# Cache moves issued by ScalarE during the projection instead of by SyncE during prompt attention

## The chip, the cores and the metric

The kernel runs on one core of a Trainium2 chip. The metric is the device time of one execution in microseconds. The core has five engines that run their own instruction streams and meet only through semaphores: TensorE (PE; its weight loads are shown apart, as PEld), VectorE (DVE), ScalarE (ACT), GpSimd (POOL) and SyncE (SP, used only to issue DMAs). 16 DMA engines move the data; each issuing engine has a queue of its own for them (q1 is SyncE's, q10 ScalarE's, q0 GpSimd's).

## The reference

One decoder layer is run for a prompt of 512 tokens and for 8 samples of 4 new tokens each that share the weights. All tokens are normed and multiplied by one wide matrix, `w_in`; its columns are the queries, keys and values of a sparse attention (NSA) and of three dilated attention groups, and the merge gates. Attention over the prompt, attention of the samples over their caches, an output projection and a mixture of experts follow.

What matters here is the last thing that the layer returns: every sample's window caches, shifted by the four new tokens (of the dilated groups; the NSA window is treated alike):

```python
buf = jnp.concatenate([dil_caches[g][l], jnp.stack([k, v], axis=2)], axis=1)
...
dil_s[g].append(buf[:, -n_buf:])
```

Rows 4 to w of each cache go unchanged to rows 0 to w-4 of the output. This copy depends on nothing that the layer computes. It is 46.9 MB in all: for one sample 4088 KB (2048 window), 1016 KB (512), 248 KB (128) and 508 KB (NSA window).

## The kernel before

The kernel is written engine by engine: within a stage, a `Block`, each engine has its own list of instructions, and every order between engines is a semaphore written out by hand. The engines meet at the end of a block. The stages that matter, in order of time:

- **Norm and transpose** (0 to 30 us). Beside it SyncE loads x, the first two chunks of `w_in` and tables; ScalarE loads a gain and the identity matrix (L598, L599).
- **Projection**, `project` (30 to 243 us). The columns of `w_in` up to the merge gates are cut into 11 chunks of 328 columns. Chunks come in pairs: `u` is 0 or 1, `k` counts the turns; a loop of 5 turns does both, and one chunk follows it. For each chunk SyncE loads 1312 KB in rows of 1312 bytes (L299, `load`), into one of two buffers `w[:, u]`; it waits until the chunk before in the same `u` is multiplied. VectorE splits the chunk into an upper part and a rest (L112 and L116, called by `split`). TensorE multiplies five token tiles (four of 128 tokens, one of 32) with three products each (L122 to L124), into eight PSUM banks used round and round. ScalarE and VectorE copy the banks into `rows` in turns (`copies`, L346; ScalarE the even ones: three copies in a chunk of `u` 0, two in one of `u` 1).
- **Merge gates and rotation**, `finish_rows` (243 to 370 us): the last 2048 columns in 16 loads of 512 KB, with the rows' rotation beside them.
- **Prompt attention**, `prompt_nsa` (370 to 552 us) and `prompt_dilated` (552 to 663 us).
- **Sample attention**, the mixing and the experts, whose weights are the largest traffic of the kernel.

The order inside VectorE's loop in `project` matters for the steps below:

```python
with dve.Fori(0, TURNS) as i:
    split(1, i)
    copies(dve, 1, dve.tensor_copy, s_dve, 0, i)
    split(0, i + 1)
    copies(dve, 1, dve.tensor_copy, s_dve, 1, i)
```

Before a chunk with `u` 0, TensorE waits for all copies of the turn before on both engines (`s_act` and `s_dve` at 5k).

The cache moves are DMAs from DRAM to DRAM, made by `move_cache` (L567 to L576; its DMA stands as L574 in the profile). It lays one sample's window out as (pieces, y) with y of at most 1024 elements. SyncE issues them: in `prompt_nsa` two samples' 2048 window in each of four turns of its loop, in `prompt_dilated` the other three windows of four samples in each of two turns. Nothing waits for them but the end of the kernel (`s_moved`, L2706).

Of the kernel before, what the change touches and what calls it, by code (L numbers as in the profile page):

```python
# [12 lines left out]
TP, BS, SS = 512, 8, 4  # L13
# [4 lines left out]
HD, NH, KVH, REP = 64, 8, 2, 4  # L18
# [64 lines left out]
CREDIT = 1  # L83
# [27 lines left out]
def upper_part(dve, out, src):  # L111
    return dve.tensor_copy(out, src)  # L112


def rest_part(dve, out, whole, upper):
    return dve.tensor_tensor(out, whole, upper, ALU.subtract)  # L116


def product_of_parts(pe, out, lhsT, rhs, first, last):

    a, b = lhsT, rhs
    pe.matmul(out, a[0], b[0], start=first, stop=False)  # L122
    pe.matmul(out, a[0], b[1], start=False, stop=False)  # L123
    return pe.matmul(out, a[1], b[0], start=False, stop=last)  # L124
# [6 lines left out]
class Program:  # L131
# [144 lines left out]
    def project(self, hT, hT_rest, w, wu, wr, s_w, rows, src, tables_loaded):  # L276

        nc = self.nc  # L280
        w_in = self.i["w_in"][0]
        TURNS = C_MRG // WCH // 2
        KV_TURNS = -(-(C_KC + 4 * HD) // (2 * WCH))
        with ExitStack() as s:
            acc = self.ps(s, "proj_acc", [P, 8, 512])
            s_up = self.lsem("w_in_upper_ready")
            s_sp = self.lsem("w_in_split")
            s_mm = [self.lsem(f"proj_accumulated{u}") for u in range(2)]
            s_act = self.lsem("proj_copied_by_act")
            s_dve = self.lsem("proj_copied_by_dve")  # L290
            s_src = self.lsem("compressor_source_copied")
            self.s_mw = [self.sem(f"merge_w_loaded{j}") for j in range(MERGE_RING)]
            self.credit()
            with nc.Block() as block:
                @block.sync
                def _(sp):
                    def load(u, k):
                        sp.wait_ge(s_mm[u], (NT + 1) * k + CREDIT)
                        sp.dma_start(w[:, u, :, :], w_in[:, bass.ds((2 * k + u) * WCH, WCH)]  # L299
                                     .rearrange("(k p) c -> p k c", p=P)).then_inc(s_w[u], 16)  # L300

                    with sp.Fori(0, TURNS - 1) as i:
                        load(0, i + 1)
                        load(1, i + 1)
                    load(0, TURNS)
                    for m in range(MERGE_RING):
                        self.load_merge_w(sp, m)
                    sp.wait_ge(s_act, 5 * KV_TURNS + CREDIT)
                    sp.wait_ge(s_dve, 5 * KV_TURNS + CREDIT)
                    for t in range(NT):  # L310
                        for kg in range(4):
                            c = C_KC + kg * HD
                            sp.dma_start(src[8 * t:8 * t + 8, kg], rows[:, t, c:c + HD]).then_inc(s_src, 16)
                    sp.wait_ge(s_src, 16 * 4 * NT + CREDIT)
                    tables_loaded(sp)

                @block.tensor
                def _(pe):
                    def chunk(u, k):
                        pe.wait_ge(s_sp, 2 * k + u + 1 + CREDIT)  # L320
                        if u == 0:
                            pe.wait_ge(s_act, 5 * k + CREDIT)
                            pe.wait_ge(s_dve, 5 * k + CREDIT)
                        for t in range(NT + 1):
                            n = 5 * u + t
                            if n >= 8:
                                pe.wait_ge((s_act, s_dve)[(n - 8) % 2], 5 * k + (n - 8) // 2 + 1 + CREDIT)
                            tok = slice(t * P, t * P + ROWS[t])
                            for c in range(KD):
                                ins = product_of_parts(pe, acc[:ROWS[t], n % 8, 0:WCH],  # L330
                                                       (hT[:, c, tok], hT_rest[:, c, tok]),
                                                       (wu[:, u, c, :], wr[:, u, c, :]), c == 0, c == KD - 1)
                            ins.then_inc(s_mm[u], 1)

                    with pe.Fori(0, TURNS) as i:
                        chunk(0, i)
                        chunk(1, i)
                    chunk(0, TURNS)

                def copies(eng, which, copy, done, u, k):  # L340

                    for t in range(NT + 1):
                        n = 5 * u + t
                        if n % 2 == which:
                            eng.wait_ge(s_mm[u], (NT + 1) * k + t + 1 + CREDIT)
                            copy(rows[:ROWS[t], t, bass.ds((2 * k + u) * WCH, WCH)],  # L346
                                 acc[:ROWS[t], n % 8, 0:WCH]).then_inc(done, 1)

                @block.scalar
                def _(act):  # L350
                    with act.Fori(0, TURNS) as i:
                        for u in range(2):
                            copies(act, 0, act.copy, s_act, u, i)
                    copies(act, 0, act.copy, s_act, 0, TURNS)

                @block.gpsimd
                def _(pool):
                    self.bias_steps[0](pool)

                @block.vector  # L360
                def _(dve):
                    def split(u, k):

                        dve.wait_ge(s_w[u], 16 * k + 16 + CREDIT)
                        upper_part(dve, wu[:, u], w[:, u]).then_inc(s_up, 1)
                        dve.wait_ge(s_up, 2 * k + u + 1 + CREDIT)
                        rest_part(dve, wr[:, u], w[:, u], wu[:, u]).then_inc(s_sp, 1)

                    split(0, 0)
# [5 lines that stand above are left out]
                    copies(dve, 1, dve.tensor_copy, s_dve, 0, TURNS)  # L375
# [409 lines left out]
    def prompt_nsa(self, rows, qrot, kcT, vc, o_tok):  # L785
# [9 lines left out]
        with ExitStack() as s:  # L795
# [22 lines left out]
            s_qt = self.lsem("pn_q_transposed")  # L818
# [19 lines left out]
            with nc.Block() as block:  # L838
# [80 lines left out]
                @block.sync  # L919
                def _(sp):  # L920
                    sp.dma_start(self.ks[:, :], self.c["sample"]).then_inc(s_ks, 16)
                    sp.wait_ge(s_z, 1 + CREDIT)
                    for i in range(NT):
                        sp.dma_start(vcz[32 * i:32 * i + NC, i, :], vc[:, :]).then_inc(s_vz, 16)
                    with sp.Fori(0, REP) as r:
                        sp.wait_ge(s_qt, 2 * r + 2 + CREDIT)
                        for j in range(BS // REP):
                            self.move_cache(sp, "cache_dil_w2048", "dil2048_sample", BS // REP * r + j)
                    sp.wait_ge(s_ks, 16 + CREDIT)

                @block.gpsimd
# [116 lines left out]
    def prompt_dilated(self, rows, o_tok):  # L1048
# [6 lines left out]
        with ExitStack() as s:  # L1055
# [13 lines left out]
            s_qt = self.lsem("pd_qk_transposed")  # L1069
# [16 lines left out]
            with nc.Block() as block:  # L1086
                @block.sync
                def _(sp):
                    with sp.Fori(0, 2) as jp:
                        sp.wait_ge(s_qt, 6 * jp + 6 + CREDIT)  # L1090
                        for j in range(BS // 2):
                            for src, dst in (("cache_dil_w512", "dil512_sample"), ("cache_dil_w128", "dil128_sample"),
                                             ("cache_nsa_win", "nsa_win_sample")):
                                self.move_cache(sp, src, dst, BS // 2 * jp + j)
                    sp.wait_ge(self.s_rows_out, 16 * self.n_rows_out)

                @block.gpsimd
# [1855 lines left out]
```

## Time and profile before

| | us |
|---|---|
| median of 3 runs | 1530.58 |
| lowest and highest run | 1524.55, 1533.27 |
| the profiled execution | 1536.05 |
| its span, first to last instruction | 1534.2 |
| TensorE busy in the span | 1211.8 (79%) |
| VectorE, ScalarE, GpSimd busy | 519.4, 296.9, 112.5 |
| data moved by DMA | 280.05 MB |

How to read it: "busy" is the time in which an engine has an instruction under way; the DMA share is the mean busy share of the 16 DMA engines; the granted clock of TensorE is given as a share of full speed, 1.00 for 2.4 GHz and 0.50 for 1.2 GHz. A packet is what the trace records as one piece of a transfer on one DMA engine; the completion of a DMA adds one small packet for each engine. A DMA's "landing" is counted from its issue to the semaphore that says that all of it has arrived. An idle engine costs nothing unless something on the path waits for it.

### The profile page before, as it was taken

What the parts mean: (1) busy time and instruction counts of PE and PEld (TensorE: products, weight loads), DVE (VectorE), ACT (ScalarE), POOL (GpSimd) and SP (SyncE); (2) the same over time, 40 slices, a digit from 0 to 9 for tenths busy, and PEclk for the clock granted to TensorE, in tenths of its full rate; (3) what the DMA queues carried; (4) which work ended last, traced back from release to release, by engine and by line L of the source; (5) the groups of instructions that cost most, each with busy time, mean ns of one, the idle gap of its engine ahead of it and who ended that gap; (6) DMA issues with size and microseconds to landing.
All of it is one profiled execution on the core that took longest, in us unless ns stands there. A gap on an engine that the chain in (4) does not pass through costs nothing. (4 is left out here: it accounts for less than half of the span.)

```text
span 1534.2 us, 21060 instructions
## 1 busy us (share of the span) xinstructions
PE 1211.8 (79%) x7946; PEld 913.0 (60%) x7946; DVE 519.4 (34%) x1053; ACT 296.9 (19%) x652; POOL 112.5 (7%) x173
## 2 busy tenths in 40 slices
PE   3999998996887777887649966995799749988760
PEld 2999998996666656646528754865575423333320
DVE  6222323141555545543413243234231341101105
ACT  3000002311333322312203222232001101101102
POOL 1400005000000020000000000000000001111100
PEclk9999999898799989967769987997799859999985
DMA  7122242263666632525652222220572369999955
GB/s 223 48 84 80 70 91 67 88 189 107 220 218 218 218 122 69 189 110 220 274 219 111 111 96 126 111 110 0 219 254 125 140 254 419 423 424 423 425 222 188
DMA packets 74629, 280.05 MB, mean 183 GB/s; under 512 B 16772, under 2 KB 45216, under 8 KB 61728
## 3 DMA queue, kind: packets, MB, share of 16 engines
q1 hardware_dynamic: 66144, 231.55, 41.3%
q0 software_dynamic: 5824, 42.48, 6.9%
q10 hardware_dynamic: 2592, 5.05, 0.9%
q8 instruction: 49, 0.80, 0.2%
q14 instruction: 20, 0.16, 0.0%
HBM read 264.80 MB, written 69.53 MB: 218 GB/s over the span
## 5 line engine op out<-in xcount | busy, mean ns | idle before, releaser
L122 PE MATMUL proj_acc<-w_in_upper,hT_upper 128*128 128x328 f32 (+1 forms) x440 | 139.2, 316 | 10.9 <-DVE w_in_rest L116 7.1
L2519 PE MATMUL ex_up_ps<-ex_w_up,ex_hT 128*64 128x512 f32 x512 | 125.2, 645 | 28.1 <-DMA ex_w_up<-in_expert_w_up 27.1
L123 PE MATMUL proj_acc<-w_in_rest,hT_upper 128*128 128x328 f32 (+1 forms) x440 | 139.1, 316 | 0.0
L124 PE MATMUL proj_acc<-w_in_upper,hT_rest 128*128 128x328 f32 (+1 forms) x440 | 138.1, 314 | 0.0
L722 PE MATMUL sn_hp<-sn_xT,cmp_w 128*128 128x127 f32 x1024 | 118.2, 275 | 0.0
L722 PEld LDWEIGHTS sn_hp<-sn_xT,cmp_w 128*128 128x128 f32 x1024 | 116.2, 192 | 0.0
L2519 PEld LDWEIGHTS ex_up_ps<-ex_w_up,ex_hT 128*64 128x64 f32 x512 | 41.5, 148 | 100.6 <-issue 90.1
L122 PEld LDWEIGHTS proj_acc<-w_in_upper,hT_upper 128*128 128x128 f32 (+1 forms) x440 | 76.7, 174 | 16.0 <-issue 12.6
L122 PE MATMUL merge_ps<-hT_upper,merge_w_upper 128*128 128x272 f32 x256 | 77.7, 303 | 4.1 <-DVE merge_w_rest L116 4.1
L123 PEld LDWEIGHTS proj_acc<-w_in_rest,hT_upper 128*128 128x128 f32 (+1 forms) x440 | 76.8, 175 | 3.6
L124 PEld LDWEIGHTS proj_acc<-w_in_upper,hT_rest 128*128 128x128 f32 (+1 forms) x440 | 76.7, 174 | 3.7
L123 PE MATMUL merge_ps<-hT_rest,merge_w_upper 128*128 128x272 f32 x256 | 77.0, 301 | 0.0
L124 PE MATMUL merge_ps<-hT_upper,merge_w_rest 128*128 128x272 f32 x256 | 76.8, 300 | 0.0
L2540 PE MATMUL ex_down_ps<-ex_w_down,ex_actT 128*64 128x512 f32 x256 | 58.4, 597 | 2.0 <-DMA ex_w_down<-in_expert_w_down 1.4
L2614 DVE TENSOR_TENSOR ex_act<-ex_silu,ex_up_ps 128x256 f32<-128x256 f32 x16 | 6.7, 421 | 155.2 <-ACT ex_silu L2570 155.2
L2051 PE MATMUL mx_ps<-mx_w_out,mx_mixT 128*128 128x512 f32 x128 | 56.2, 594 | 1.0 <-DVE mx_products L2142 1.0
L895 PE MATMUL pn_O<-rows,pn_pT 128*128 128x128 f32 x320 | 44.6, 288 | 13.8 <-DVE pn_pT L1003 13.8
L863 PE MATMUL pn_S<-pn_kT,pn_qT 128*128 128x128 f32 (+3 forms) x128 | 51.0, 514 | 5.0 <-ACT pn_qT L951 5.0
L122 PEld LDWEIGHTS merge_ps<-hT_upper,merge_w_upper 128*128 128x128 f32 x256 | 51.5, 201 | 4.6 <-DVE merge_w_rest L116 4.4
L895 PEld LDWEIGHTS pn_O<-rows,pn_pT 128*128 128x128 f32 x320 | 39.5, 197 | 23.4 <-DVE qrot_and_o_tok L1040 18.9
L2039 PE MATMUL mx_ps<-oT,mx_w 128*128 128x272 f32 x192 | 45.9, 403 | 8.2 <-DMA mx_w<-in_w_branch_dil 8.2
L124 PEld LDWEIGHTS merge_ps<-hT_upper,merge_w_rest 128*128 128x128 f32 x256 | 51.6, 201 | 0.0
(429 smaller groups left out, 1945.3 us busy)
## 6 DMA issues: line engine op xcount, KB each, us to landing
ex_w_up<-in_expert_w_up SPq DMA_DIRECT2D x32, 2048.0 KB, 28.0
ex_w_down<-in_expert_w_down SPq DMA_DIRECT2D x32, 1024.0 KB, 35.7
out_dil_sample<-in_cache_dil_w SPq DMA_DIRECT2D x8, 4088.0 KB, 21.4
sd_kv<-in_cache_dil_w SPq DMA_DIRECT2D x16, 1024.0 KB, 11.8
w_in_chunk<-in_w_in SPq DMA_DIRECT2D x11, 1312.0 KB, 5.7
merge_w<-in_w_in SPq DMA_DIRECT2D x16, 512.0 KB, 5.1
out_dil_sample<-in_cache_dil_w SPq DMA_DIRECT2D x8, 1016.0 KB, 10.1
merge_gates_scratch<-qT_dil ACTq DMA_DIRECT2D x16, 272.0 KB, 4.2
```

What stands on the lines that cost most here:

```text
L122: pe.matmul(out, a[0], b[0], start=first, stop=False)
L123: pe.matmul(out, a[0], b[1], start=False, stop=False)
L124: return pe.matmul(out, a[1], b[0], start=False, stop=last)
L722: ins = pe.matmul(b["hp"][kg % 2][:, 0:n - 1], self.w1[:, kg // 2, j, :], b["xT"][:, kg % 2, j % 8, j // 8:j // 8 + n - 1], start=j == 0, ...
L863: pe.matmul(S[bf][:, j, 0:n], qT[:, 1, g, i * P:(i + 1) * P], kT[:, j, 0:n], start=True, stop=False)
L895: pe.matmul(O[u % 2][:, j * P:(j + 1) * P], pT[:, j, kb * P:(kb + 1) * P], rows[:, kb, c:c + KVD], start=kb == 0, stop=kb == i)
L2039: ins = pe.matmul(ps[:, 4 * (m % 2) + 2 * p + half, 0:HT], w[:, c0 + k, m * P:(m + 1) * P], oT[:, c0 + k, half * HT:(half + 1) * HT], star ...
L2051: ins = pe.matmul(ps[:, n % 3, :], mixT[:, k, t * P:(t + 1) * P], wo[:, k, half * 512:(half + 1) * 512], start=k == 0, stop=k == KD - 1)
L2519: ins = pe.matmul(up_ps[r, q, :], hT[:, q, c, r], wu[slot][:, u, c, :], start=c == 0, stop=c == KD - 1)
L2540: ins = pe.matmul(dn_ps[r, half, :], aT[:, q, c, r], wd[slot][:, u, c, half * 512:(half + 1) * 512], start=c == 0, stop=c == 1)
L2614: dve.tensor_tensor(ac[:, q, :], sl[:, q, :], up_ps[:, q, FF:2 * FF], ALU.mult).then_inc(s_ac, 1)
```

## The change

ScalarE issues all 32 moves, on its own queue, in the projection: four DMAs (one sample) ahead of each group of copies, for the first eight chunks. Its loop has four turns instead of five, and the fifth is written out. The two loops of moves on SyncE are gone. `move_cache` is as before and is called with ScalarE in the place of SyncE. The number of moves, the data and the final wait are the same.

```diff
--- before.py
+++ after.py
@@ -348,9 +348,16 @@
 
                 @block.scalar
                 def _(act):
-                    with act.Fori(0, TURNS) as i:
+                    MOVED = (("cache_dil_w2048", "dil2048_sample"), ("cache_dil_w512", "dil512_sample"),
+                             ("cache_dil_w128", "dil128_sample"), ("cache_nsa_win", "nsa_win_sample"))
+                    with act.Fori(0, BS // 2) as i:
                         for u in range(2):
+                            for from_cache, to_cache in MOVED:
+                                self.move_cache(act, from_cache, to_cache, 2 * i + u)
                             copies(act, 0, act.copy, s_act, u, i)
+                    for k in range(BS // 2, TURNS):
+                        for u in range(2):
+                            copies(act, 0, act.copy, s_act, u, k)
                     copies(act, 0, act.copy, s_act, 0, TURNS)
 
                 @block.gpsimd
@@ -922,10 +929,6 @@
                     sp.wait_ge(s_z, 1 + CREDIT)
                     for i in range(NT):
                         sp.dma_start(vcz[32 * i:32 * i + NC, i, :], vc[:, :]).then_inc(s_vz, 16)
-                    with sp.Fori(0, REP) as r:
-                        sp.wait_ge(s_qt, 2 * r + 2 + CREDIT)
-                        for j in range(BS // REP):
-                            self.move_cache(sp, "cache_dil_w2048", "dil2048_sample", BS // REP * r + j)
                     sp.wait_ge(s_ks, 16 + CREDIT)
 
                 @block.gpsimd
@@ -1086,12 +1089,6 @@
             with nc.Block() as block:
                 @block.sync
                 def _(sp):
-                    with sp.Fori(0, 2) as jp:
-                        sp.wait_ge(s_qt, 6 * jp + 6 + CREDIT)
-                        for j in range(BS // 2):
-                            for src, dst in (("cache_dil_w512", "dil512_sample"), ("cache_dil_w128", "dil128_sample"),
-                                             ("cache_nsa_win", "nsa_win_sample")):
-                                self.move_cache(sp, src, dst, BS // 2 * jp + j)
                     sp.wait_ge(self.s_rows_out, 16 * self.n_rows_out)
 
                 @block.gpsimd
```

## Rows read from the trace of the kernel before

**Rows 1.** busy us (share of the span) and instructions by engine, from the page.
```profile
PE 1211.8 (79%) x7946; PEld 913.0 (60%) x7946; DVE 519.4 (34%) x1053; ACT 296.9 (19%) x652; POOL 112.5 (7%) x173
```

**Rows 2.** busy time in stretches: projection, merge gates, prompt attention, experts.
```profile
core 0: us, PE busy (x) PEld busy (x) DVE busy (x) ACT busy (x) POOL busy (x), PEclk, DMA share, GB/s
30.00:243.00 213.00, 202.19 (x1320) 189.67 (x1320) 63.80 (x49) 12.10 (x29) 22.70 (x20) 1.00 0.24 71
243.00:370.00 127.00, 122.71 (x940) 122.03 (x940) 41.18 (x69) 29.84 (x59) 22.71 (x60) 0.93 0.41 123
370.00:552.00 182.00, 135.61 (x856) 107.85 (x856) 93.28 (x301) 61.01 (x181) 8.58 (x12) 0.87 0.58 194
1255.00:1492.00 237.00, 203.74 (x918) 78.30 (x914) 26.92 (x47) 28.71 (x63) 31.74 (x37) 0.94 0.91 380
```

**Rows 3.** waits of TensorE from 370 to 663 us: total us, times, longest.
```profile
PE pn_O L895 <- DVE pn_pT L1003: 13.8, 12, 1.4
PE pn_O L909 <- DVE pn_cmp_exp L1024: 12.8, 4, 3.2
PE pn_PT L854 <- DMA pn_cmp_v_by_tile<-prompt_vc: 8.1, 1, 8.1
```

**Rows 4.** timeline of ScalarE in the projection: start us, us, what [idle before].
```profile
56.02 0.42 ACT L346 COPY rows<-proj_acc 32x328 f32 x1 [6.75 <-PE proj_acc L124]
70.45 0.43 ACT L346 COPY rows<-proj_acc 128x328 f32 x1 [6.75 <-PE proj_acc L124]
78.66 0.43 ACT L346 COPY rows<-proj_acc 128x328 f32 x1 [7.77 <-PE proj_acc L124]
115.69 0.43 ACT L346 COPY rows<-proj_acc 128x328 f32 x1 [7.79 <-PE proj_acc L124]
```

**Rows 5.** timeline of VectorE in the projection, the split of one chunk.
```profile
61.82 1.53 DVE L112 CAST w_in_upper<-w_in_chunk 128x2624 fp32r<-128x2624 f32 x1 [8.85 <-DMA w_in_chunk<-in_w_in]
63.38 2.89 DVE L116 TENSOR_TENSOR w_in_rest<-w_in_chunk,w_in_upper 128x2624 fp32r<-128x2624 f32 x1
```

**Rows 6.** the loads of w_in by line: issue ns, first, last start; landing.
```profile
L299 SPq DMA_DIRECT2D w_in_chunk<-in_w_in x9: 372/373/397, 56.1 to 204.0; - x9
DMA to landing us min/median/max: 5.6/5.7/6.0
```

**Rows 7.** the Exp of prompt attention, 471-497 us, then 497-508 us.
```profile
L959 ACT ACTIVATE pn_exp<-pn_S,pn_stats x13: 358/474/689, 472.7 to 496.9; 128x128 f32<-128x128 f32 x4, 128x256 f32<-128x256 f32 x4, 128x384 f32<-128x384 f32 x3, 128x512 f32<-128x512 f32 x2
...
L959 ACT ACTIVATE pn_exp<-pn_S,pn_stats x4: 572/630/688, 496.9 to 500.9; 128x384 f32<-128x384 f32 x2, 128x512 f32<-128x512 f32 x2
```

**Rows 8.** the moves by line; the first two in the queue's timeline.
```profile
L574 SPq DMA_DIRECT2D out_dil_sample<-in_cache_dil_w x24: 520/521/657, 385.0 to 621.0; - x24
...
384.96 1.52 SPq L574 DMA_DIRECT2D out_dil_sample<-in_cache_dil_w  x2
```

**Rows 9.** SyncE's queue, 384-415 us, 562-588 us; one us after an issue.
```profile
q1 hardware_dynamic: 160, 8.37, 82.5%
...
q1 hardware_dynamic: 384, 7.26, 83.5%
...
384.90:385.90 1.00, 0.00 (x0) 0.00 (x0) 0.37 (x1) 0.99 (x2) 0.98 (x2) 0.50 0.00 0
```

**Rows 10.** SyncE's queue, 57 to 62 us: packets, MB, share of 16 engines.
```profile
q1 hardware_dynamic: 1040, 1.34, 77.2%
```

**Rows 11.** both queues, 6.5 to 7.5 us: packets, MB, share of 16 engines.
```profile
q1 hardware_dynamic: 99, 0.36, 89.5%
q10 hardware_dynamic: 98, 0.05, 16.4%
```

**Rows 12.** busy time and granted clock (after POOL) around a pause of TensorE.
```profile
912.00:925.80 13.80, 0.18 (x1) 0.00 (x0) 11.35 (x13) 2.12 (x2) 0.79 (x1) 0.50 0.96 411
925.80:931.80 6.00, 5.37 (x45) 4.48 (x49) 1.96 (x6) 1.17 (x2) 0.00 (x0) 0.50 0.90 388
931.80:936.00 4.20, 3.71 (x125) 3.04 (x116) 0.35 (x1) 0.00 (x0) 0.00 (x0) 1.00 0.02 4
```

## The prediction

> **What bounds the kernel now.** I read the busy time and the clock by stage first. TensorE is busy over the whole span for 79% [rows 1], but the stage that receives the moves is tighter than that: in the projection (30 to 243 us) it works 202 of 213 us at the full clock, while the DMA engines are used to 24%; in prompt attention (370 to 552 us), from which the moves are taken, it works 136 of 182 us, with the DMA engines at 58%; the experts (1255 to 1492 us) are the only stage that the DMA engines bound, at 91% [rows 2]. So transfers are to go from a stage where an engine has idle time into one where TensorE has almost none. The question is then what each stage waits for.
>
> In prompt attention the waits of TensorE name other engines: 13.8 us for VectorE's probabilities, 12.8 us for the compressed ones. The one DMA wait, 8.1 us, is for a small load that TensorE needs before the loop in which the moves stand [rows 3]. No wait names a cache move.
>
> In the projection one turn of the loop (two chunks of w_in) takes 37.03 us: ScalarE's first copy of a turn stands at 78.66 and again at 115.69 us [rows 4]. A chunk is five token tiles of 3.6 us (two of ScalarE's copies, two tiles apart, are 7.2 us apart). The load of the chunk after next is issued as a chunk ends (56.1 us; the last copy of that chunk starts at 56.02), lands 5.7 us later, and VectorE splits it in 4.4 us (61.82 to about 66.2 us) [rows 4 to 6]. It is needed at 75.0 us (the copy at 78.66 less one tile of 3.6). So a load has 8.8 us of cover at most, and it can take up to about 14.5 us from issue to landing before TensorE notices. That cover is what the change uses.
>
> **Part by part.** *Taken from SyncE.* 8 moves of the 2048 window in prompt attention and 24 smaller ones in the dilated part, with their two waits. SyncE has nothing else to do there, and nothing else is queued behind them (the next load of its queue is issued after the moves have landed). What this gives back: nothing on the path. The Exp of 128x512 takes at most 689 ns with moves under way (471 to 497 us) and 688 ns without (497 to 508 us) [rows 7], so the attention's engines are not slowed by them. Bounds: 0 to 5 us, taken 0; zero is what these rows are nearest to.
>
> *Given to ScalarE, the issuing.* Four DMAs ahead of each of the first eight groups of copies. SyncE needs 0.52 us for one issue, and some 0.25 us of register work lies between two of them (two issues in 1.52 us) [rows 8]: about 3.1 us a group. ScalarE sits idle 6.75 to 7.79 us before every copy [rows 4], so this is hidden: 0. Behind the issues stand the copies that free the PSUM banks; without the cover it would be 8 x 3.1 = 25 us, and that would need the queue to push back. Seven packets a queue and sample, below, speak against it. The peeled turn has the same copies as the looped one: 0.
>
> *The transfers themselves.* This is the term that decides, and it needs the size of packets. Two 2048 moves are 160 packets, 8.37 MB; 32 of the packets are the 16 completions of each, so 128 packets carry 65 KB each, 8 on each of 16 engines. They use the engines for 82.5% of 31 us = 25.6 us, so 3.2 us a packet. Four samples' smaller moves (12 DMAs) are 384 packets, 192 of them data, 3 an engine and sample, and use 83.5% of 26 us = 21.7 us, 5.4 us a sample [rows 9]. One sample is thus 4 + 3 = 7 large packets and 4 x 3.2 + 5.4 = 18.2 us of every DMA engine; eight samples are 146 us. A load of w_in is 1024 data packets of 1312 bytes, 64 an engine, in 77.2% of 5 us = 3.9 us, 0.06 us a packet [rows 10]. Both together, 22.1 us, are already more than a chunk of 18.5 us.
>
> How two queues share an engine is seen at 6.5 to 7.5 us, where ScalarE's queue (512-byte rows of the identity) and SyncE's (4 KB rows of x) are both full: 98 packets of one and 99 of the other in 1 us, 0.05 against 0.36 MB [rows 11]. So they take turns packet by packet, whatever the size. Beside the moves a w_in packet of 0.06 us then waits for a move packet of 3.2 us. A load gets 64 turns only if the moves end before.
>
> **One turn, followed.** Times are those of the turn at 56 us. The load is issued at 56.1 and its first packet runs 1.3 us later (5.7 less 3.9, less 0.5 for the completion), at 57.4. ScalarE ends its last copy at 56.4, issues at about 56.7, and the first move packet runs at 58.0, if it needs the same 1.3 us (no byte moved in the first 0.9 us after such an issue [rows 9]). Ten packets of the load are through by then. The sample's 7 packets last until 58.0 + 18.2 + 0.4 = 76.6 us, and 7 of the load pass with them. But ScalarE issues the next sample after its copy at 70.45 us [rows 4], at about 71.2, and these packets stand ready at 72.5, 4 us before the queue would run dry. So 7 more packets of moves go first, until 95.2 us; the load has had 24. The other 40 take 2.4 us: it lands at 98.1. VectorE splits until 102.5, then makes the three copies that stand behind the split in its order (1.6 us; TensorE waits for them before a new turn), and TensorE starts at 104.1 instead of 75.0 us: **29.1 us** lost. The other chunk's load, queued behind, lands at 102 and is split by 108.5, ahead of 122, so it costs nothing. The third sample is issued only after the delayed chunk, so that the next turn repeats this from its own start. This holds for three turns; in the fourth only one sample (the eighth) stands against the load: the moves end at 76.6 in the same frame, the load, 47 packets short, lands at 79.9, and TensorE starts at 85.9: 10.9 us. Sum 3 x 29.1 + 10.9 = **98 us**.
>
> *The clock.* After 13.8 us in which TensorE did almost nothing the granted clock was 0.50, the 1.2 GHz level, and it stayed there for the first 6.0 us of work before it returned to 2.4 GHz [rows 12]. At half speed that is 3 us for each long stall, 9 us, and I take 2 for the short one: **11 us**.
>
> *The rest.* The first sample is issued at about 30 us, when no load of w_in is on its way; it stretches the compressor's weight loads, for which only GpSimd waits, long before the merge stage needs its product: 0. The last sample is through before the ninth chunk starts, so the merge stage (96% busy [rows 2]) and its loads meet no moves: 0. Later stages are as before.
>
> The sum is +109 us: 1536.05 us for the profiled execution (its span is 1534.2) becomes 1645, and on the median of the runs, 1530.58, **1640 us**.
>
> **Rivals.** (1) The queues take turns, but the load gets through in a few turns. Against it are the 98 and 99 packets of [rows 11]; for it, that this row has packets of at most 4 KB. If it waited for four move packets, it would land at about 58.0 + 12.8 + 3.2 + 0.5 = 74.5 and TensorE start at 80.5, 5.5 us late; four turns, each with something for the second load too, are 15 to 35 us. If it waited for one sample but never for two (were the moves 25% faster, the queue would run dry first), it is 4 x 11 + 8 = 52 us. So 1546 to 1583 us, about 1560 in the middle. The Trainium skill has such a rule: "DMA: Bandwidth & Descriptors", section "Queues, rings and completion order", says that an engine drains a packet of typically 9 to 17 descriptors from one ring before it switches. If each packet of this trace were one of its descriptors, an estimate from that page is four to six turns for a load, the first of these two cases. The trace at 6.5 to 7.5 us shows one for one and does not agree.
>
> (2) The load is hardly delayed: the large packets are cut up and bytes are shared fairly. A load of 3.9 us then takes about 8 and lands within 10 us of its issue, inside the 14.5. Then TensorE sees nothing, and what the moves lag behind (8 x (22.1 - 18.5) = 29 us) is absorbed by the last three chunks. 1531 to 1536, about 1533 us. Against it: nothing in the rows shows a packet interrupted, and the moves' packets keep an engine 3.2 us each, one behind the other.
>
> (3) Faster: the moves do cost something in prompt attention that its waits do not name. The place is the first 26 us of each of its four turns and the 22 us after each issue of the small moves; were the chain 5% slower there, it would be 4 x 1.3 + 2 x 1.1 = 7.4 us, 1523 us, and only if rival 2 held as well. It decides from about 5% on. The two equal Exp durations speak against it [rows 7].
>
> (4) The moves don't run there at all, because ScalarE's queue takes them late: with seven packets an engine and sample there is no reason. It would end as rival 2 and has no chance of its own.
>
> **The numbers.** My forecast 0.65, with 1605 to 1670 of its own (a stall of 25 to 33 us, with and without the clock); rival 1 0.20; rival 2 0.10; rival 3 0.05. The range takes the forecast's upper end and most of rival 1: 1555 to 1670 us. About 0.5%, 7.7 us, is what a measurement of this kernel can tell from no change. Faster by more: 0.04; within: 0.11; slower: 0.85.
>
> **What would show it.** Right: in the projection, TensorE waits of some 29 us, three times, and one of 11, put down to VectorE's copies or split, which wait for the w_in load; landing of every second w_in load at about 42 us instead of 5.7; a granted clock of 0.50 after each stall; packets of 65 KB on ScalarE's queue (q10), 46.9 MB there; ScalarE's issues at 0.5 us each; prompt attention within 2 us of before. Wrong: w_in loads that land in under 14 us (then rival 2), or in about 18 (rival 1); issues on ScalarE of many us each, with its copies late (then the issuing was the term that I set at 0); a shorter prompt attention (rival 3). The sum hangs on the next sample's being issued 4 us before the queue runs dry; a small shift there is worth 18 us a turn.

## The result

| | before | changed |
|---|---|---|
| median of the runs (4 each) | 1529.84 us | 1637.41 us |
| range of the runs | 1524.55 to 1533.27 | 1634.94 to 1638.95 |
| ratio to before, 95% interval | 1 | 1.0683 [1.0657, 1.071] |
| span of the profiled execution | 1534.2 us | 1635.7 us |

The changed kernel is 7% slower: 107.6 us by the medians, 101.5 us by the spans of the two profiled executions (that of before lay some 6 us above its median).

The page of the changed kernel, busy time and queues:

```profile
PE 1212.1 (74%) x7946; PEld 915.2 (56%) x7946; DVE 517.1 (32%) x1053; ACT 296.6 (18%) x652; POOL 111.3 (7%) x173
...
q1 hardware_dynamic: 64736, 183.54, 30.1%
q10 hardware_dynamic: 4000, 53.05, 9.3%
```

TensorE is busy for as long as before [rows 1]; only its share has fallen. The moves now stand on q10, which carried 5.05 MB before; the 48.0 MB between are the 46,880 KB of 1024 bytes that the text ahead of the prediction calls 46.9 MB. By stretches (projection, merge gates, the two parts of prompt attention):

```profile
core 0: us, PE busy (x) PEld busy (x) DVE busy (x) ACT busy (x) POOL busy (x), PEclk, DMA share, GB/s
30.00:350.60 320.60, 209.48 (x1320) 197.02 (x1320) 61.98 (x50) 12.12 (x29) 22.32 (x20) 0.83 0.61 197
350.60:472.20 121.60, 117.32 (x940) 116.65 (x940) 40.91 (x69) 29.78 (x59) 21.89 (x60) 0.97 0.44 129
472.20:653.80 181.60, 136.03 (x856) 108.12 (x856) 93.27 (x301) 60.92 (x181) 7.90 (x12) 0.87 0.03 9
653.80:764.70 110.90, 88.14 (x536) 69.14 (x536) 54.95 (x161) 30.00 (x86) 8.62 (x13) 0.91 0.00 1
```

Against [rows 2]: the projection takes 320.6 instead of 213 us, with 7.3 us more of busy time at a mean clock of 0.83; the merge stage takes 5 us less, at 0.97 instead of 0.93; the first part of attention takes what it took, 182 us, though its DMA share has fallen from 58% to 3%, and the second 110.9 us where it took 111. So the whole loss is in the projection, and nothing came back where the moves were taken away.

The waits tell what holds TensorE up there. These are its waits for a late chunk in the projection of the changed kernel (total, times, longest; three are of 30.3 to 30.7 us, one of 11.9 and one of 0.8):

```profile
PE proj_acc L122 <- DVE rows L346: 104.2, 5, 30.7
```

The loads of w_in, from issue to landing:

```profile
DMA to landing us min/median/max: 5.9/28.2/42.7
```

VectorE's timeline in the first turn that meets the moves (start, duration, in brackets what it waited for):

```profile
98.41 1.53 DVE L112 CAST w_in_upper<-w_in_chunk 128x2624 fp32r<-128x2624 f32 x1 [45.82 <-DMA w_in_chunk<-in_w_in]
99.97 2.89 DVE L116 TENSOR_TENSOR w_in_rest<-w_in_chunk,w_in_upper 128x2624 fp32r<-128x2624 f32 x1
102.78 1.29 DVE L346 COPY rows<-proj_acc 128x328 f32 x3
```

ScalarE's timeline in the same turn:

```profile
70.07 0.43 ACT L346 COPY rows<-proj_acc 128x328 f32 x1 [6.78 <-PE proj_acc L124]
70.65 2.07 ACTq L581 DMA_DIRECT2D out_dil_sample<-in_cache_dil_w  x3
73.05 0.53 ACTq L581 DMA_DIRECT2D out_nsa_win_sample<-in_cache_nsa_win  x1
110.07 0.43 ACT L346 COPY rows<-proj_acc 128x328 f32 x1 [39.57 <-PE proj_acc L124]
```

Followed backwards: ScalarE waits for TensorE, TensorE for VectorE's copies, these stand behind the split, and the split waits 45.8 us for a load of w_in. That load took 42.7 us where it took 5.7 [rows 6]. ScalarE's four issues take 2.6 us of engine time and end 37 us before its next copy can begin; they are not on the path.

How the two queues share the engines, from 66 to 72 us of the changed kernel (packets, MB, share of 16 engines):

```profile
q10 hardware_dynamic: 42, 1.89, 101.7%
q1 hardware_dynamic: 42, 0.06, 3.4%
```

These are 42 packets of moves and 42 of the load, 1.89 against 0.06 MB. The queues take turns one for one, as at 6.5 us of before [rows 11], now with 45 KB on average (65 KB in the largest) against 1.3 KB.

### The profile page after: what moved, and what is told of

Read it like the earlier page. It is cut to its first block and busy times, and to the rows that moved or that the text cites. A ratio compares the mean times of both kernels' runs of the same rounds, so it can differ in the third digit from the quotient of the medians.

```text
span 1635.7 us, 21030 instructions
## 1 busy us (share of the span) xinstructions
PE 1212.1 (74%) x7946; PEld 915.2 (56%) x7946; DVE 517.1 (32%) x1053; ACT 296.6 (18%) x652; POOL 111.3 (7%) x173
## 5 line engine op out<-in xcount | busy, mean ns | idle before, releaser
L122 PE MATMUL proj_acc<-w_in_upper,hT_upper 128*128 128x328 f32 (+1 forms) x440 | 142.9, 325 | 111.3 <-DVE rows L346 104.2
L2516 PEld LDWEIGHTS ex_up_ps<-ex_w_up,ex_hT 128*64 128x64 f32 x512 | 41.5, 148 | 100.3 <-issue 89.8
L112 DVE CAST w_in_upper<-w_in_chunk 128x2624 fp32r<-128x2624 f32 x11 | 16.7, 1518 | 173.9 <-DMA w_in_chunk<-in_w_in 172.9
L346 ACT COPY rows<-proj_acc 128x328 f32 (+3 forms) x28 | 12.1, 431 | 308.9 <-PE proj_acc L124 308.9
```

The lines of the kernel that those rows point to most:

```text
L2516: ins = pe.matmul(up_ps[r, q, :], hT[:, q, c, r], wu[slot][:, u, c, :], start=c == 0, stop=c == KD - 1)
```

## The experiments

**One sample against the load instead of two.** `second_group_only` and `first_group_only` issue the samples of one group of copies in the projection and leave the other four to SyncE in prompt attention. `issued_later` has all eight, and issues the first group's sample one copy later. The first diff is the edit of the two half-sized kernels in the projection, the second that of `issued_later`.

```diff
 for u in range(2):
-    for from_cache, to_cache in MOVED:
-        self.move_cache(act, from_cache, to_cache, 2 * i + u)
+    if u == 1:   # second_group_only; u == 0 in first_group_only
+        for from_cache, to_cache in MOVED:
+            self.move_cache(act, from_cache, to_cache, 2 * i + u)
```

```diff
 for u in range(2):
+    copies(act, 0, act.copy, s_act, u, i, range(1 - u))
     for from_cache, to_cache in MOVED:
         self.move_cache(act, from_cache, to_cache, 2 * i + u)
-    copies(act, 0, act.copy, s_act, u, i)
+    copies(act, 0, act.copy, s_act, u, i, range(1 - u, NT + 1))
```

> Only the samples of the second group of copies (odd ones, issued as a chunk with u 0 ends, together with its load) are moved by ScalarE in the projection; the four others by SyncE in prompt attention, one in each of its four turns. Theory (turns, 64 KB packets): each load of a u 0 chunk waits for one sample, not two: 11 us lost in each of four turns, with the slow clock 1582 us. Rival (bandwidth): the DMA engines need 18.2 + 7.8 = 26 us of the 37 us of a turn, nothing is lost: 1530 us.

> Only the samples of the first group of copies (even ones, issued 3.3 us before a chunk with u 1 ends) are moved by ScalarE in the projection, the others by SyncE in prompt attention. Theory (turns): now it is the load of the u 1 chunk that finds one sample ahead of it. It is issued about 2 us after the first move packet, waits for some 6 of the 7, and is needed a chunk later: about 6.5 us lost in three turns (the first sample meets no load), with some slow clock 1550 to 1556 us. Rival (bandwidth): 1530 us.

> The changed kernel, but ScalarE issues the first group's sample behind that group's first copy instead of ahead of it, so that it comes only when the chunk runs. Same bytes, same queue, same number of issues. Theory: the queue of moves runs dry before the next sample comes, the load waits for one sample and the tail of another, not for two: about 15 us lost in each of four turns, with the slow clock about 1600 us. Rival (bandwidth or issuing): 1637 us as the changed kernel, since nothing but the moment of one issue differs.

Measured, one timed execution each: second_group_only 1582.76 us, first_group_only 1555.2 us, issued_later 1607.52 us. TensorE's wait on the late chunk and the landing of the loads, in that order of kernels:

```profile
PE proj_acc L122 <- DVE rows L346: 48.7, 5, 12.7
DMA to landing us min/median/max: 6.1/10.2/24.7
```

```profile
PE proj_acc L122 <- DVE w_in_rest L116: 28.9, 4, 7.5
DMA to landing us min/median/max: 5.9/7.4/21.8
```

```profile
PE proj_acc L122 <- DVE rows L346: 71.1, 5, 17.9
DMA to landing us min/median/max: 6.0/15.4/29.9
```

The waits of before are 3.9 us for the copies and 7.1 us for the first split; less these, the three kernels lose 44.8 us in four turns, 21.8 us in three and 67.2 us in four. Half the bytes cost half as much or a fifth of the changed kernel's 100.3 us, by which load they stand against, where the DMA engines had room for all of them (their share of the projection is 46 and 51%). issued_later moves every byte that the changed kernel moves and is 30 us faster; single executions of the kernel before lay between 1523.8 and 1537.45 us, so 30 us is well clear of their spread. That refutes bandwidth as the cause, and it bears out the detail on which the sum hung: in the changed kernel the second sample joins the queue before it runs dry.

**The same bytes in one queue.** `one_queue` puts the sample behind the load, on SyncE, and takes the moves from ScalarE (not shown):

```diff
-with sp.Fori(0, TURNS - 1) as i:
-    load(0, i + 1)
-    load(1, i + 1)
+with sp.Fori(0, TURNS - 1) as i:
+    for u in range(2):
+        load(u, i + 1)
+        for from_cache, to_cache in MOVED:
+            self.move_cache(sp, from_cache, to_cache, 2 * i + u)
```

> The same eight samples in the same eight chunks of the projection, but issued by SyncE behind each load of w_in, so that loads and moves stand in one queue, in order. The bytes and the packets of 65 KB are those of the changed kernel. Theory (in one queue there are no turns; a load waits only for the sample issued before it): the DMA engines need 18.2 + 3.9 = 22.1 us a chunk of 18.5, a load lands 3.6 us later each time (5.7, 9.7, 13.3 us ...) until the cover of 14 us is used up, and the other chunks then run at 22.1 us: about 20 us lost in all, 1550 us. Rival (the loss is in sharing the DMA engines at all): 1637 us.

Measured: 1543.56 us. Its waits and landings:

```profile
PE proj_acc L122 <- DVE rows L350: 11.4, 5, 3.7
PE proj_acc L122 <- DVE w_in_rest L116: 9.8, 3, 7.1
...
DMA to landing us min/median/max: 5.9/15.3/18.0
```

TensorE waits 10 us more than before, not 100. This is what the DMA engines' limit costs by itself; the other 90 us of the changed kernel come from the second queue. My 20 us were too many: VectorE's splits of the first and the ninth of these chunks begin at 60.69 and 229.30 us, so a load and a sample together took 21.1 us a chunk and not 22.1, and the loss is then 8 x (21.1 - 18.5) less the 8.8 us of cover, 12 us. What makes the pair 1 us shorter than its parts was not separated.

The issues themselves were not free in this queue (ns, minimum, median and maximum):

```profile
L581 SPq DMA_DIRECT2D out_dil_sample<-in_cache_dil_w x24: 520/866/7052, 55.4 to 200.9; - x24
```

One of them took up to 7.1 us, where it took at most 0.66 us before [rows 8]. It cost little here, since SyncE has nothing else to do; on ScalarE the copies would have stood behind it.

**The price of issuing, and of the moves where they were.** `issue_only` lets ScalarE issue four DMAs of 62 KB a group; `no_moves` is before without the moves, whose copied rows it leaves out.

```diff
+for quarter in range(4):
+    self.move_quarter(act, "cache_dil_w128", "dil128_sample", 2 * i + u, quarter)
 copies(act, 0, act.copy, s_act, u, i)
```

> The kernel before, but ScalarE issues four DMAs ahead of each of the first eight groups of copies in the projection as in the changed kernel; they are small (quarters of one sample's 128 window, one packet of 4 KB an engine each), the other windows stay on SyncE in prompt attention. Theory: issuing is hidden by ScalarE's idle 7 us before each copy: 1530 us, within 3 us. Rival (issuing on ScalarE delays the copies and so TensorE): up to 8 x 3.1 = 25 us more, 1555 us.

> The kernel before without the 32 cache moves: the copied rows of the four sample caches are left out, and nothing waits for them. Theory (the moves cost nothing in prompt attention, so there was nothing to win by taking them away): the same as before, 1530 us, within 3 us. Rival (they cost what the waits don't name): faster by 5 us or more, and prompt attention (370 to 663 us) shorter by as much.

The time as a ratio to before, with its interval: issue_only 1.001 [0.9989, 1.0031], no_moves 1.0006 [0.9987, 1.0024]. Neither differs from before by more than 0.3%. Prompt attention of no_moves (367.1 to 550 us):

```profile
367.10:550.00 182.90, 135.79 (x856) 107.92 (x856) 93.26 (x301) 61.26 (x182) 7.48 (x12) 0.87 0.03 11
```

136 us busy of 183, as with the moves [rows 2]. Without any moves the kernel is at most 0.13%, 2 us, faster. So another placement has no more than that to win from what the moves cost where they are; whether one could win in another way, by the granted clock say (last section), this does not tell.

**The size of the moves' packets.** `pack16k`, `pack8k` and `pack4k` take the pieces of a cache in an order in which no two that follow each other touch, so that each piece stays a packet of its own (the diff is shortened; the 4097 of 16 KB is 2049 for 8 KB and 1025 for 4 KB):

```diff
-y = max(d for d in range(1, 1025) if n % (P * d) == 0) if n % P == 0 else n // 16
-flat = "b w c h d -> b (w c h d)"
+y = max(d for d in range(1, 4097) if n % (16 * d) == 0)
+flat, turned = "b w c h d -> b (w c h d)", "b (r s y) -> s (b r) y"
```

> The changed kernel, but each move's rows are taken in an order in which no two neighbours touch, so that its packets are at most 16 KB instead of 65 KB; bytes, queue and place of issue are the same. One sample is then 16 + 4 + 1 + 2 = 23 packets an engine instead of 7. Theory (the queues take turns, packet by packet): a load of w_in has 64 packets an engine, 10 of them ahead; two samples still hold only 46 turns, so the load still lands when both are through: no change from the changed kernel, 1637 us. Rival (bytes are shared, the loss is bandwidth): 1637 us too, but then at 8 KB and 4 KB as well.

> The same with packets of 8 KB: 46 packets of 0.40 us a sample. Theory: 54 turns of 0.46 us, the load lands at about 83 us instead of 98, TensorE loses 14 us a turn instead of 29 in the first three turns, 11 in the fourth, with the slow clock 1592 us. Rival (bandwidth): 1637 us.

> The same with packets of 4 KB: 92 packets of 0.20 us a sample. Theory: 54 turns of 0.26 us, the load lands at about 72.5 us, 3 to 6 us lost a turn: 1545 to 1570 us. With 92 packets an engine and sample ScalarE's queue may push back, and then its issues take more than 0.5 us and its copies come late; the two are told apart by ScalarE's issue times. Rival (bandwidth): 1637 us.

Measured: 16 KB 1565.08 us, 8 KB 1634.76 us, 4 KB 1678.79 us (ratio 1.095 [1.0915, 1.0984]). All three miss, the first to the better, the others to the worse. By its time alone pack8k even fits the rival that it was to refute (bandwidth, 1637 us); what speaks is the count of packets. q10 and q1 from 66 to 72 us with 16, 8 and 4 KB:

```profile
q10 hardware_dynamic: 93, 1.52, 83.0%
q1 hardware_dynamic: 93, 0.12, 12.2%
```

```profile
q10 hardware_dynamic: 141, 1.15, 86.0%
q1 hardware_dynamic: 140, 0.18, 8.1%
```

```profile
q10 hardware_dynamic: 251, 0.98, 78.6%
q1 hardware_dynamic: 252, 0.33, 26.8%
```

It is one for one at every size. What I had wrong were two other sizes. The first is the load's head start, which explains the 16 KB. These are q1 from 55 to 58 us, then q10 and q1 from 58 to 60 us, of the changed kernel:

```profile
q1 hardware_dynamic: 152, 0.20, 32.0%
...
q10 hardware_dynamic: 14, 0.92, 105.7%
q1 hardware_dynamic: 487, 0.64, 86.3%
```

By 60 us the load has moved 639 packets, 40 an engine, while most engines run their first move packet; I had reckoned with 10. Of its 64 packets an engine, 24 are left. With 7 or 14 large packets ahead that makes no difference, since the load waits for all of them anyhow; with 23 packets of 16 KB a sample the load is through after about 24 turns instead of 46. TensorE's waits in pack16k:

```profile
PE proj_acc L122 <- DVE w_in_rest L116: 25.0, 4, 9.0
PE proj_acc L122 <- DVE rows L346: 14.7, 5, 9.1
```

Less those of before these are 28.7 us, against 100.3. This is the sharpest of the tests, though its number was missed: bytes, queue, place of issue and the rate of the moves (next) are those of the changed kernel, only the packets are more and shorter, and 72 us are gone.

The second is the rate of the moves, read while nothing else is moved (35 to 50 us, before the next load of w_in is issued): 16, 8 and 4 KB, in this order, and the changed kernel last.

```profile
q10 hardware_dynamic: 338, 4.89, 101.4%
```

```profile
q10 hardware_dynamic: 402, 3.29, 101.2%
```

```profile
q10 hardware_dynamic: 547, 2.24, 117.5%
```

```profile
q10 hardware_dynamic: 143, 4.92, 96.2%
```

In 15 us these are 326, 219, 149 and 328 GB/s. A packet of 8 KB costs 0.6 instead of 0.4 us, and one sample of 6 MB takes 27 us, more than a chunk of 18.5; the load of the other chunk comes late as well. With pieces this small the DMA engines' rate does bind, beside the turns. At 4 KB the queue also pushes back. ScalarE's issues in pack4k (ns, minimum, median and maximum), then its first turn:

```profile
L581 ACTq DMA_DIRECT2D out_dil_sample<-in_cache_dil_w x24: 598/2952/34902, 30.5 to 327.8; - x24
```

```profile
55.02 27.95 ACTq L581 DMA_DIRECT2D out_dil_sample<-in_cache_dil_w  x3
83.21 5.03 ACTq L581 DMA_DIRECT2D out_nsa_win_sample<-in_cache_nsa_win  x1
```

Three issues take 28 us, where they take 2.1 us in the changed kernel, and ScalarE's copies stand behind them.

In these kernels the engines take neighbouring pieces in turn, so that size and order were mixed. `near8k` and `near4k` give each DMA engine its own stretch of the cache again, every second piece in one DMA and the others in a second.

```diff
+for half in range(2):
+    sp.dma_start(dst.rearrange(flat)[bass.ds(b, 1), 0:n].rearrange(turned, s=16, h=2, y=y)[:, :, half, :],
...
+# turned = "b (s h r y) -> s (b r) h y"
```

> The changed kernel with packets of 8 KB as in pack8k, but each DMA engine reads its own stretch of the cache: every second row in one DMA, the others in a second one, eight DMAs a sample instead of four. In pack8k the engines took neighbouring rows in turn, and the moves alone ran at 221 GB/s instead of 330. Question: did the small size or that order slow them? If the order: 330 GB/s again, 0.40 us a packet; a load of w_in has some 40 of its 64 packets an engine through before the first move packet runs (the changed kernel's trace), the other 24 take 24 x 0.46 = 11 us, it lands some 17 us after its issue, 2 to 4 us lost a turn: 1535 to 1555 us. If the size: 1635 us as pack8k.

> The same with 4 KB packets, as pack4k (151 GB/s alone, and ScalarE's issues took up to 38 us for three). If the order slowed the moves there: 330 GB/s alone and the load lands some 8 us after the first move packet, nothing lost by turns; with 92 packets an engine and sample the queue still pushes back on ScalarE's issues, for up to the length of one sample (18 us), so 1540 to 1600 us. If the size: 1679 us as pack4k.

Measured: 1617.58 and 1663.53 us. The moves alone, 35 to 50 us, 8 KB and then 4 KB:

```profile
q10 hardware_dynamic: 429, 3.38, 101.7%
```

```profile
q10 hardware_dynamic: 567, 2.25, 107.5%
```

These are 225 and 150 GB/s, against 219 and 149: of the two orders tried neither matters for the rate, the size of the pieces does. The times lie 17 and 15 us below those of pack8k and pack4k, so the order is not without effect on the rest. For near8k, TensorE waits 12.6 us less in the projection and is busy 5.8 us less in the merge stage (last section); why it waits less was not tried.

## Why the prediction was right, and where it was not

The forecast was 1640 us, 110 more than before; measured are 1637.41. Term by term:

- **The mechanism.** The queues take turns packet by packet, and the load waits for both samples. This is shown by the 42 against 42 packets, by the half-sized and shifted variants and by pack16k. The first turn came out as worked out: landing at 98.4 us (98.1), TensorE's start at 104.2 us (104.1).
- **The stalls.** 98 us predicted; 104.2 less 3.9 = 100.3 us measured. By turns, less the 0.8 us of before, these are 29.9, 29.7, 29.5 and 11.1 us (29.1 three times and 10.9). The term that was mis-sized inside it is the head start of the load, 40 packets instead of 10: the first move packets run between 59.5 and 60 us, 3.6 us or more after their issue at 55.88, and I had given them the 1.3 us of the load. That the landing still fits is partly luck. The moves began 1.5 to 2 us later than in the sum, which puts their end as much later, and the 30 packets more that the load had through by then are worth 1.8 us (30 x 0.06) the other way. The same slip cost the expectation of pack16k 72 us.
- **The time of a sample.** 18.2 us predicted. The moves alone ran 4.92 MB in 15 us, so the 6.0 MB of a sample take about 18.3 us as long as nothing else moves. With a load beside it a sample and a load took 21.1 us and not 22.1 (one_queue).
- **The clock.** 11 us predicted; TensorE is busy 7.3 us longer in the projection. The end of the first stall and the work behind it (busy time by engine, granted clock, DMA share):

```profile
74.00:104.20 30.20, 0.00 (x0) 0.02 (x1) 5.76 (x6) 0.00 (x0) 0.00 (x0) 0.56 0.84 282
104.20:108.50 4.30, 4.29 (x16) 4.30 (x17) 4.19 (x2) 0.00 (x0) 0.00 (x0) 0.51 0.00 0
108.50:112.00 3.50, 3.50 (x25) 3.50 (x24) 0.00 (x0) 0.43 (x1) 0.00 (x0) 1.00 0.00 0
```

  The clock stays at the 1.2 GHz level for 4.3 us of work here, not for the 6.0 us of [rows 12].
- **The merge stage, set at 0.** It is 5 us shorter, at a clock of 0.97 instead of 0.93. The prediction did not see this, and it makes good most of the slow clock in the projection. Its cause is open, and with one traced execution of each kernel it may not be the change's doing at all; the last section has what the other kernels show.
- **Issuing on ScalarE, set at 0.** This is shown by issue_only, 1.001 [0.9989, 1.0031]. It holds for the few packets that the prediction named as its condition; in pack4k, with 92 an engine and sample, the issues are no longer hidden.
- **Taking the moves from attention, set at 0.** This is shown by no_moves, 1.0006 [0.9987, 1.0024]. Rival 3 falls with it.
- **Rival 1** falls with the counts of 42 and 42, 93 and 93. Its own case "one sample, but never two", priced at 52 us, is what second_group_only built: 1582.76 us, 52 us above the median of before. **Rival 2** falls with the landing of 42.7 us.

The sum of the terms that were off, +2 for the stalls, -4 for the clock and -5 for the merge stage, is -7 us, and by the traced executions the forecast is indeed 7.5 us too high: 1645 against 1637.48. Taken over to the medians it is only 3 us off, because the traced execution of before lay 6 us above its median and that of the changed kernel at its own. That part of the agreement is luck.

## What to carry to other kernels

Before a bulk copy goes onto a second queue beside loads that something waits for, count packets, not bytes: the load's packets an engine, against the number and length of the copy's packets that can stand in the other queue while it runs. In the first turn here, a load that had 24 small packets an engine still to come waited for all 14 large ones, 36 us of them. Put the copy behind the load in the same queue, on an engine that has nothing else to do (10 us of waits instead of 100 here), or leave it where no load is urgent. And ask first what the move would free: prompt attention, whose waits named none of the moves, gained nothing when they went.

## What the runs showed of the hardware

- DRAM-to-DRAM copies slow down with small pieces, in both orders tried: 328 GB/s at 65 KB, 326 at 16 KB, 219 to 225 at 8 KB and 149 to 150 at 4 KB. Pieces of 4088 bytes that touch each other were moved as packets of 65 KB, so that the shape written in the code does not say which of these holds.
- The push-back of a full queue lands on the engine that issues. With 92 packets an engine and sample one issue on ScalarE took up to 34.9 us (pack4k) and 17.7 us (near4k); with 46 (pack8k, near8k) it took at most 0.77 us. On SyncE's queue, where each sample of 7 stood behind a load of 64, it took up to 7.1 us (one_queue). At what number a queue pushes back was not measured.
- The merge stage is the same 940 matmuls in all of these kernels, but its granted clock differs. TensorE is busy in it for 122.7 us (before), 122.5 (no_moves) and 122.4 (issue_only), where nothing was added to the waits of the projection. In the kernels that wait longer there it is 116.7 (one_queue), 117.3 (changed), 117.4 (second_group_only), 119.3 (pack16k), 119.8 (pack4k), 120.6 (first_group_only and near4k), 120.7 (issued_later), but 122.5 in near8k and 128.3 in pack8k. The stage in no_moves, second_group_only and pack8k, in this order:

```profile
244.30:367.10 122.80, 122.48 (x940) 121.76 (x940) 39.09 (x67) 27.39 (x56) 20.63 (x58) 0.93 0.43 125
```

```profile
297.70:415.40 117.70, 117.40 (x940) 116.72 (x940) 39.17 (x68) 27.37 (x55) 19.81 (x58) 0.98 0.45 130
```

```profile
341.40:470.10 128.70, 128.28 (x940) 127.51 (x940) 39.01 (x68) 27.50 (x56) 19.72 (x58) 0.88 0.41 119
```

  The difference is time at the lower level in the midst of full work, not after a pause. The same stretch of the stage in before and in the changed kernel:

```profile
275.00:305.00 30.00, 30.00 (x201) 29.96 (x200) 5.84 (x11) 8.68 (x13) 0.00 (x0) 0.77 0.30 91
```

```profile
382.50:412.50 30.00, 30.00 (x251) 29.79 (x251) 8.44 (x17) 9.93 (x15) 0.00 (x0) 1.00 0.41 117
```

  TensorE is busy for all of the 30 us in both, and gets through 201 matmuls in one and 251 in the other. It is tempting to say that pauses in the projection buy this back. The kernels don't bear it out: one_queue, with 10 us more of waits, has the most, issued_later, with 67 us, little, near8k, with 75 us, nothing, and pack8k, with 88 us, the reverse. Each is one traced execution, and executions of the kernel before differ by 14 us among themselves. What sets the clock there is open.
